# Weight splits of a float32 decoder trunk on whole slabs of 2048 columns instead of halves of 1024

## What is computed

```python
for layer in range(DEPTH):                       # DEPTH = 2
    xn = rmsnorm(h, norm_mix[layer])
    h = h + (even_mixer(xn, ...) if layer % 2 == 0 else odd_mixer(xn, ...))
    h = h + cross_attention(rmsnorm(h, norm_xattn[layer]), memn, xa_wq[layer], xa_wkv[layer], xa_wo[layer])
    h = h + sq_relu_mlp(rmsnorm(h, norm_mlp[layer]), mlp_w1[layer], mlp_w2[layer])
return rmsnorm(h, norm_final)

def fox_attention(q, k, v, f_logit):             # the softmax that the prediction speaks of
    s = q @ k^T * scale + c_i - c_j              # c: cumulative log forget gate; causal
    return softmax(s) @ v
def sq_relu_mlp(xn, w1, w2):
    return jnp.square(jax.nn.relu(xn @ w1)) @ w2
```

## Time and profile before

| | |
|---|---|
| time, median of 3 runs | 2406.83 us (2405.9 to 2407.12) |
| profiled execution: its time, its span | 2407.2 us, 2405.4 us |
| PE busy | 2392.7 us, 99% of the span |
| DVE, ACT, POOL busy | 1490.1, 1187.7, 356.5 us |
| PE clock granted | tenths of full speed: 9 in each of the 40 slices (9 is 90% or more); 1.00 in each stretch asked for up to 2396 us |
| weights and the rest from HBM | 471.5 MB, 204 GB/s over the span |

### The profile page before, as it was taken

One profiled execution on the slowest core, in us unless ns is written; L12 is line 12 of the kernel. 1 busy time (PEld: TensorE's weight loads), 2 busy tenths in 40 slices (PEclk: granted clock), 3 DMA queues, 4 the chain that ended last, 5 costly groups with the idle time before them and its releaser, 6 DMA issues.

```text
span 2405.4 us, 31978 instructions
## 1 busy us (share of the span) xinstructions
PE 2392.7 (99%) x12516; PEld 2021.8 (84%) x12516; DVE 1490.1 (62%) x1872; ACT 1187.7 (49%) x1580; POOL 356.5 (15%) x482
## 2 busy tenths in 40 slices
PE   9999999999999999999999999999999999999998
PEld 7878888889888888888888888888888888888887
DVE  5546554556665557888866657566755655555556
ACT  7544455546544444444445445556644444444444
POOL 0033120100564002554610100000000000000000
PEclk9999999999999999999999999999999999999999
DMA  8655565574566567787786768864665565566563
GB/s 311 215 171 188 182 203 174 163 205 144 191 193 191 190 195 225 238 259 234 252 276 191 224 211 258 266 201 149 202 193 191 188 191 189 187 190 192 191 192 123
DMA packets 338359, 488.56 MB, mean 203 GB/s; under 512 B 18948, under 2 KB 181668, under 8 KB 338116
## 3 DMA queue, kind: packets, MB, share of 16 engines
q1 hardware_dynamic: 312836, 460.42, 60.7%
q0 software_dynamic: 4256, 14.02, 2.1%
q10 hardware_dynamic: 21152, 12.53, 1.7%
HBM read 471.52 MB, written 19.60 MB: 204 GB/s over the span
## 4 chain that ended last, share of the span: by engine, by line
PE 96%; DVE 2%; ACT 1%; issue 0%; DMA 0%; ACTq 0%; SPq 0%; DVEq 0%
PE acc L635 20%; PE acc L637 19%; PE acc L636 19%; PE acc L1111 18%; PE acc L1108 9%; PE tp L702 2%; PE at L726 2%; PE acc L1076 1%; PE at L1076 1%; DVE wlo L1854 1%; PE tp L726 1%; PE acc L985 1%; PE acc L983 1%; PE acc L984 1%; ACT whi L1282 1%; PE at L1079 0%
## 5 line engine op out<-in xcount | busy, mean ns | idle before, releaser
L1854 DVE TENSOR_TENSOR wlo<-raw,whi 128x1024 fp32r<-128x1024 f32 x824 | 1047.9, 1275 | 795.1 <-ACT whi L1282 792.5
L1282 ACT ACTIVATE whi<-raw 128x1024 fp32r<-128x1024 f32 x824 | 870.1, 1060 | 975.7 <-PE acc L637 577.4
L635 PE MATMUL acc<-whi,yt_hi 128*128 128x512 f32 x1408 | 553.1, 393 | 0.2 <-DVE arena L2236 0.2
L637 PE MATMUL acc<-whi,yt_lo 128*128 128x512 f32 x1408 | 548.4, 390 | 0.0
L636 PE MATMUL acc<-wlo,yt_hi 128*128 128x512 f32 x1408 | 548.3, 389 | 0.0
L1111 PE MATMUL acc<-x,whi 128*128 128x512 f32 x1984 | 485.6, 392 | 0.0
L1111 PEld LDWEIGHTS acc<-x,whi 128*128 128x128 f32 x1984 | 361.4, 189 | 68.5 <-issue 0.8
L635 PEld LDWEIGHTS acc<-whi,yt_hi 128*128 128x128 f32 x1408 | 264.4, 188 | 56.4 <-issue 1.6
L637 PEld LDWEIGHTS acc<-whi,yt_lo 128*128 128x128 f32 x1408 | 264.3, 188 | 55.7
L636 PEld LDWEIGHTS acc<-wlo,yt_hi 128*128 128x128 f32 x1408 | 264.5, 188 | 53.1
L1108 PEld LDWEIGHTS acc<-x,wlo 128*128 128x128 f32 x1984 | 262.8, 191 | 15.3 <-issue 0.8
(11 more groups left out here) (246 smaller groups left out, 1556.5 us busy)
## 6 DMA issues: line engine op xcount, KB each, us to landing
raw<-in_mlp_w SPq DMA_DIRECT2D x256, 1024.0 KB, 5.6
raw<-in_ab_w_in SPq DMA_DIRECT2D x56, 1024.0 KB, 5.0
raw<-in_cd_w_in SPq DMA_DIRECT2D x32, 1024.0 KB, 5.5
raw<-in_ab_w_out SPq DMA_DIRECT2D x16, 1024.0 KB, 5.2
raw<-in_cd_w_out SPq DMA_DIRECT2D x16, 1024.0 KB, 7.2
raw<-in_xa_wkv SPq DMA_DIRECT2D x15, 1024.0 KB, 9.8
raw<-in_xa_wq SPq DMA_DIRECT2D x16, 512.0 KB, 4.7
raw<-in_xa_wo SPq DMA_DIRECT2D x8, 512.0 KB, 4.6
```

Source lines behind the costliest of these rows:

```text
L635: pe.matmul(a, xh, whi[:, w, kk], start=opens and kk == 0, stop=False)
L637: last = pe.matmul(a, xl, whi[:, w, kk], start=False, stop=closes and kk == 1)
L1282: act.activation(split_weights(whi, kind, i), half_weights(raw, kind, i), ACT.Copy)\
L1854: dve.tensor_tensor(split_weights(wlo, kind, i), half_weights(raw, kind, i), split_weights(whi, kind, i).bitcast(F32), ALU.subtract).then_ ...
```

## The change

ACT splits a whole slab in one instruction of 2048 columns, and DVE computes the slab's `wlo` in one, for the kinds "full", "wide", "pair", "seq" and "heads" from the second unit on. "query", "mixed" and unit 0 keep halves. The rings keep their size, so they hold two slabs: ACT now waits, ahead of halves i and i + 1 (i even), until halves up to i - 3 have been used (`p.at("half", i - RING + 2)`), which frees both places. The counters go up by 2 where they went up by 1. PE's, SP's and POOL's programs are as before.

```diff
+        def whole_slab(kind, unit):
+            return kind not in ("query", "mixed") and unit > 0
+        def slab_raw(kind, i):
+            v = raw[:, i // 2].rearrange("p a n -> p (a n)")
+            return v.rearrange("p (k h n) -> p h k n", k=8, h=2) if kind == "heads" else v
+        def slab_split(t, kind, i):
+            v = t[:, i % RING:i % RING + 2].rearrange("p h a n -> p (h a n)")
+            return v.rearrange("p (h k n) -> p h k n", k=8, h=2) if kind == "heads" else v
...
+                if whole_slab(kind, p.n["unit"]):
+                    if i % 2 == 0:
+                        act.wait_ge(half_used, p.at("half", i - RING + 2))
+                        act.activation(slab_split(whi, kind, i), slab_raw(kind, i), ACT.Copy).then_inc(hi_ready, 2)
+                    return
                 if p.n["half"] + i >= RING or p.reg is not None:
                     act.wait_ge(half_used, p.at("half", i - RING + 1))
...
-                    dve.wait_ge(hi_ready, p.at("half", i + 1))
-                    dve.tensor_tensor(split_weights(wlo, kind, i), half_weights(raw, kind, i),
-                                      split_weights(whi, kind, i).bitcast(F32), ALU.subtract).then_inc(lo_ready, 1)
+                    if not whole_slab(kind, p.n["unit"]):
+                        dve.wait_ge(hi_ready, p.at("half", i + 1))
+                        dve.tensor_tensor(split_weights(wlo, kind, i), half_weights(raw, kind, i),
+                                          split_weights(whi, kind, i).bitcast(F32), ALU.subtract).then_inc(lo_ready, 1)
+                    elif i % 2 == 0:
+                        dve.wait_ge(hi_ready, p.at("half", i + 2))
+                        dve.tensor_tensor(slab_split(wlo, kind, i), slab_raw(kind, i),
+                                          slab_split(whi, kind, i).bitcast(F32), ALU.subtract).then_inc(lo_ready, 2)
                     if slot:
                         slot(i)
```

## The result

The changed kernel takes **2546.28 us** (median of 4 runs, 2542.11 to 2549.94) against 2406.75 before: +139.5 us, ratio 1.058 with a 95% interval of 1.0567 to 1.0593. The prediction was +99, with a range of +38 to +171.

The account below looks back on a forecast made before the run. PE, busy for 99% of the span, was taken as the bound, so every wait is paid. Terms 1 to 5, 16 + 42 + 21 + 9 + 11 = 99 us, added to the median 2406.83 gave 2506 us; range 2445 to 2578.

Parts of the forecast that it names:

- The mechanism: Plain units: slab split only after half i - 3 ends (time T), ready at T + 4.42; slack falls from 5.6 to 1.0 us.
- Instruction lengths: 2048-column instructions, extended from 512 and 1024 columns: ACT's split 1.91 us, DVE's subtraction 2.28 us.
- Term 3: Softmax of forgetting attention, two groups: PE waits 4.4 us for head 0, then for later heads; 21 us.
- Term 1: Starts of MLP units: `add_block` and sums behind the slab come late, 0.2 to 0.5 us each; 16 us for twelve steps.
- Term 2: Table stage, four MLP steps with 16 chunks: late splits, DVE's parts and unit starts; 42 us.
- Term 4: Layer 1's mixer: convolution, last output parts and S5 block sums wait behind whole slabs; 9 us.
- Term 5: The rest: first whole unit, `kv` and cross attention's neighbours, forget gate, rotary, norms, last unit; 11 us.
- The clock: Rival: stalls of 3 to 4 us lower PE's clock, adding 60 to 200 us; both large-loss rivals together 0.09.
- Faster or unchanged: Rival: fewer, longer instructions let PE's matmuls come closer, up to 133 us back; chance 0.04, half each.

Follow-up runs that it names:

- e9: e3 with one more DVE instruction, a maximum over 512 columns that nothing reads, ahead of each of the 64 whole-slab subtractions; 2406.56 us.
- e10: e3 with two more DVE instructions, maxima over 512 columns that nothing reads, ahead of each of the 64 whole-slab subtractions; 2418.92 us.
- e5: Kernel before, with 1024-column instructions and each half's own wait kept, but the slots of two halves together behind the second; 2435.27 us.
- e8: Changed kernel with ACT splitting in halves of 1024 columns, each with its own wait; DVE still 2048 columns, slots still in pairs; 2478.74 us.
- e3: Kernel before, with whole slabs only for halves 4 to 7 of the units of eight plain MLP steps (64 slabs); 2407.07 us, ratio 1.0002.
- e4: Changed kernel with DVE's accumulator sums, additions and `lo_parts` ahead of a whole slab's subtraction, in MLPs and layer 1's start and last unit; 2465.75 us.
- e1: Kernel before, with whole slabs in four units only: beside the softmax of the two head groups and behind each; 2436.14 us.
- e11: e4 with halves in the four units around the softmax and in the four MLP steps with table chunks; 2423.61 us.
- e6: Changed kernel with two 1024-column instructions on both ACT and DVE, keeping the slab's one wait and its slots together; 2462.46 us.

## Why the prediction was right, and where its terms were off

- **The mechanism** (a slab anchored at the end of half i − 3, ready at T + 4.42, slack of 1.0 us in place of 5.6) was right. The trace has T + 4.5 and a slack of 0.85 to 1.0 us; e9 and e10 put it at 0.9; e5 to e8 move head 0's wait as computed. The bounds that I gave for the slack, 0.9 to 1.3, don't follow from my own lengths: with two old ones (2.12 and 2.46 us) a slab is ready at T + 4.81, and the lower bound should have been 0.6.
- **Instruction lengths** 1.91 and 2.28 us: 1.916 and, undisturbed, 2.29. The Trainium skill's figure for such a float32 operation of two tensors ("VectorE: DVE Perf Modes", § "The TRN2 errata — SBUF-src ops pay a fixed extra latency per instruction", 2291 ns) agrees. Its advice to use large tiles was no guide to the time here: in e3 it was worth nothing.
- **Term 3**, the softmax: waits of 4.5, 3.2 and 2.6 us in each group, 20.6 in all, against 4.4, 3 and 3.1, 21. The second and third end with DVE's `lo_head`, not with ACT's copy, which I had named. What the term lacked is the clock behind the waits, 8.4 us.
- **Term 1**: 28.7 us over twelve steps for 16. The place and releasers were right. The size was off: after a pair unit 0.58 us instead of 0.5, after a hidden one 0.33 to 0.43 instead of 0.2, and matmuls behind each stall add 0.1 or so. My T + 4.33 for the next DVE instruction was T + 4.42 by the trace.
- **Term 2**, the table stage: 47.2 for 42, and that it came so close is luck. I had 22 us for splits that ACT issues late behind `k_sum`, and 11 and 5.6 for parts and unit starts. In the trace between 990 and 1300 us, the waits for `wlo`, all behind such splits, are 14.3 us in 8 places (I had forecast 16 to 30 of them), and those for accumulators (L2260, L1915) 18.2. The clock, which I had at nothing, put 8.0 us where the first part fell short by 8. e4 brings the stage to 10 us by DVE's order alone, so that order is the cause of most of it, of the accumulators' waits directly and of part of ACT's lateness by way of `k_sum`. How much of the 14.3 us would stay if DVE's sum alone came on time, no run tells.
- **Term 4**: 6.1 for 9.
- **Term 5**: 31.2 for 11. Of the missing 20 us, 14 are the five transposes and 6 the clock. I had looked for what PE waits for in the slots of accumulators and softmax, not for the banks of `tp`; `lo_parts` in slot 4 of a paired order is the same case.
- **The clock**: I had made it a rival above +160 us and forecast a PEclk of 1.00. It was neither: 24 to 26 us. Shown is that it falls with PE's waits of up to 4.3 us in e1, where little else was changed, and that it is back to 0.999 in e11, where the longest wait is 2.5 us. Shorter waits are no clear case. Behind the transposes' waits of 2.6 us (by PE's idle time) it fell in some places (3.1 us in the stretch from 1300 on) and not in others (none from 470 to 635); in e4 it fell behind a wait of 1.8 us at 36 us (PEclk 0.57 from 37 to 41 us), and in e11 it stayed at 1.00 there, behind nearly the same wait. What decides stays open.
- **Faster or unchanged**, by closer matmuls: excluded by e3 at the size that I had given it.

The sum of 99 was low by the clock (24 us), the transposes (14) and the unit starts (13), and high by 8 in terms 2 and 4: 142, as the two traces have it. So the range held because it was wide, on a point that was 40 us low: what PE waits for was mostly listed rightly, and the transposes and the clock were not in the sum.

## What to carry to other kernels

When a producer's instruction is doubled over a ring of fixed size, the longer instruction costs nothing by itself as long as the item is ready in time (e3); what it delays is dear (84 of the 140 us here, from e6 to the changed kernel). Work out when the doubled item can start (its release moves later), when it ends, and what slack is left until its consumer wants it; then list everything that stands behind it on its engine and is waited for by someone, accumulators and transposition banks too. Each such thing that needs more than the slack is a stall. If only that list is late, put it ahead of the long instruction, into the time in which its engine waits anyway: here that gave back 80 of 140 us. A larger ring, which would leave more slack, was not tried.

Two items in a row that are each late by the same amount stalled their consumer once here, not twice (e10): what it had used before the stall releases the second one on time.

## What was not expected of the hardware

Stalls of PE cost more than their length. In e1, with two groups of waits of 4.3, 3 and 2.5 us each, 29 us were lost for 20.6 of waits, with the granted clock at 0.88 in the 29 us from 377 on; the changed kernel's trace, behind the same stall, has matmuls 0.43 us apart instead of 0.23. The 1.00 in the profile before (up to its tail) belonged to a PE whose longest wait was 1.3 us, and it didn't hold when PE was made to wait. And where an engine's results are ready before they are wanted, its fixed cost per instruction is free: 13.8 us less of DVE and 12.8 less of ACT in e3 left the time as it was.
